# An mLSTM layer's input projections as one-level Strassen block products on eight Trainium2 cores

## What is computed

```python
u = jnp.einsum("bsd,de->bse", x, w_in)       # w_in: 2048 x (2*1024 + 3*2048 + 16)
qk, v, o, z, gates = jnp.split(u, ...)
qk = jax.nn.silu(_causal_depthwise_conv(qk, conv_w, conv_b))   # width 4 along tokens
h = _mlstm_chunkwise(qh, kh, vh, ig_h, lf_h)  # 8 heads, key 128, value 256: recurrence over tokens
h = hc * lax.rsqrt(jnp.mean(hc * hc, axis=-1, keepdims=True) + LN_EPS)   # per head, hc = h - mean
h = h * head_g
h = jax.nn.sigmoid(o) * h * jax.nn.silu(z)    # the gates
y = jnp.einsum("bse,ed->bsd", h, w_out)
x = _layernorm(ALPHA * x + y, ln_g, ln_b)
```

## Time and profile before

| | |
|---|---|
| runs shown, median (lowest to highest) | 2603.67 us (2599.31 to 2607.32) |
| span of the profiled execution, slowest core (all eight) | 2594.3 us (2582.3 to 2594.3) |
| TensorE, VectorE, GpSimd, ScalarE busy | 97%, 61%, 41%, 34% |
| first layer's projections end, second layer begins | 970.65 us, 1192.60 us |

### The profile page before, as it was taken

How to read it: one execution, slowest core, us unless ns; L and a number is a source line. 1 busy time by engine, 2 the same in 40 slices (tenths; PEclk the granted TensorE clock), 3 DMA queues, 4 the chain that set the end, 5 groups by cost and what they waited for, 6 DMA issues and landing times.

```text
span 2594.3 us, 38771 instructions; the slowest of 8 cores (2582.3 to 2594.3 us)
## 1 busy us (share of the span) xinstructions
PE 2526.9 (97%) x13315; PEld 1274.2 (49%) x13315; DVE 1593.5 (61%) x2805; ACT 891.8 (34%) x1573; POOL 1052.5 (41%) x1006
## 2 busy tenths in 40 slices
PE   7999999999999999999899999999999999998997
PEld 3565555555555664444444444444444444443443
DVE  3755555555655555664676666666666777645665
ACT  2423333333333321322344443434334444421111
POOL 3333333333333222433554545454445555442533
PEclk9999999999999999999999999999999999999999
DMA  9878769595966469984455555655555555676762
GB/s 158 136 122 118 107 96 131 84 130 79 134 94 96 107 124 211 229 226 120 103 110 115 107 104 107 115 102 108 109 113 107 118 110 103 131 182 172 249 217 82
DMA packets 473742, 335.06 MB, mean 129 GB/s; under 512 B 413520, under 2 KB 446416, under 8 KB 461776
## 3 DMA queue, kind: packets, MB, share of 16 engines
q1 hardware_dynamic: 451984, 197.25, 34.9%
q0 software_dynamic: 21568, 135.35, 30.1%
HBM read 273.86 MB, written 92.27 MB: 141 GB/s over the span
## 4 chain that ended last, share of the span: by engine, by line
PE 91%; DVE 3%; DMA 2%; POOL 1%; issue 1%; SPq 1%; ACT 1%; DVEq 0%; ACTq 0%; POOLq 0%
PE PSA L892 31%; PE PSA L566 26%; PE PSA L731 15%; PE PSA L518 6%; PE PSA L1058 4%; PE PSA L973 4%; PE PSA L506 1%; DMA REGX<-x_t 1%; DVE REGW L1000 1%; SPq L161 1%; DMA REGX<-REGW 1%; PE PSA L619 1%; PE PSA L617 1%; POOL REGW L756 1%; PE PSA L623 1%
## 5 line engine op out<-in xcount | busy, mean ns | idle before, releaser
L892 PE MATMUL PSA<-REGH,REGX 128*128 128x512 bf16 x4096 | 978.9, 380 | 6.5 <-DVE REGW L899 6.5
L1000 DVE TENSOR_TENSOR_SCAN REGW<-PSA,REGW 128x512 f32<-128x512 f32 (+3 forms) x640 | 682.9, 1091 | 289.6 <-ACT PSA L978 235.3
L566 PE MATMUL PSA<-REGH,REGX 128*128 128x256 bf16 (+1 forms) x4096 | 701.7, 326 | 0.0
L1026 POOL TENSOR_TENSOR REGW<-REGW 128x1024 bf16<-128x1024 f32 (+7 forms) x384 | 527.4, 1391 | 329.9 <-DVE REGW L1000 177.1
L892 PEld LDWEIGHTS PSA<-REGH,REGX 128*128 128x128 bf16 x4096 | 397.8, 98 | 465.0 <-issue 12.6
L566 PEld LDWEIGHTS PSA<-REGH,REGX 128*128 128x128 bf16 x4096 | 395.8, 98 | 229.6
L978 ACT ACTIVATE PSA<-PSA 128x512 f32<-128x512 f32 (+3 forms) x640 | 327.0, 519 | 287.9 <-PE PSA L973 281.3
L904 ACT CAST REGW<-PSA 128x512 bf16<-128x512 f32 x192 | 112.6, 586 | 351.9 <-PE PSA L892 348.5
L973 PE MATMUL PSA<-REGW 128*128 128x512 bf16 (+3 forms) x640 | 220.9, 350 | 8.3 <-DVE REGW L1000 8.3
L731 PE MATMUL PSA<-REGH,REGX 128*128 128x512 bf16 x1024 | 225.7, 383 | 2.0 <-DVE REGW L734 1.1
L731 PE MATMUL PSA<-REGX,REGW 128*128 128x512 bf16 x1024 | 222.0, 379 | 1.3 <-DVE REGW L734 1.3
(11 more groups left out here) (121 smaller groups left out, 1954.3 us busy)
## 6 DMA issues: line engine op xcount, KB each, us to landing
REGX<-wb POOLq DMA_DIRECT2D x64, 512.0 KB, 4.3
y<-REGW SPq DMA_DIRECT2D x26, 1024.0 KB, 5.6
REGH<-a_wv POOLq DMA_DIRECT2D x32, 768.0 KB, 18.2
wb<-kv_w POOLq DMA_DIRECT2D x32, 512.0 KB, 10.7
wb<-b_w_in POOLq DMA_DIRECT2D x32, 512.0 KB, 9.1
REGW<-y SPq DMA_DIRECT2D x14, 1024.0 KB, 7.7
REGW<-x SPq DMA_DIRECT2D x13, 1024.0 KB, 7.0
REGH<-a_wqk POOLq DMA_DIRECT2D x16, 512.0 KB, 26.6
```

What stands on the lines that cost most here:

```text
L566: yield Op("pe", lambda: P_.matmul(PS[bank][:, 0:n1 - n0], lhsT=XT[tb][:, c, t0:t0 + 128], rhs=WV[par][:, c, n0:n1], start=(c == 0), stop= ...
L892: yield Op("pe", lambda c=c: P_.matmul(PS[bank], lhsT=WS[i % 4][:, c, :], rhs=X1[tb][:, c, :], start=(c == 0), stop=(c == KC - 1)), R=[f"W ...
L1000: yield Op("dve", lambda: V.tensor_tensor_scan(out=RR[slot][:, lo:hi][:, ::-1], data0=PS[bank][:, 0:w][:, ::-1], data1=mk[:, ::-1], initia ...
L1026: yield Op("pool", lambda: G.tensor_tensor(out=AA[:, (pos + b0) * 128:(pos + b1) * 128], in0=RR[slot][:, lo + 1:hi + 1], in1=RR[slot][:, l ...
```

## The change

- **Block products.** q, k, v, o, z all come channel-major, in pairs of 128-channel units: per head the pairs are (q, k), (v, v), (o, z), (o, z). A pair `w` with two token blocks is a 2 x 2 block product over the two halves of the 2048 channels, and `grp` makes it from seven products of 8 chunks x 512 columns instead of eight. Head 0's first two pairs stay plain (`plain`).
- **Sums.** `xsum` makes the sums of x once per token pair (and negates and subtracts in place). `wsum` makes five sums of 1024 elements for each pair of weight units, on GpSimd. `gev` evacuates a group: two copies on ScalarE, five 512-wide operations on VectorE.
- **v** is written in bf16 to four buffers `VTa` and transposed by SP's DMA into `VN` (`vtr`); the input-gate weight goes onto k instead (`knw`, ScalarE) and into the mask multiplication.
- **Gates.** `gat` makes them channel-major, with head_g, and writes them to DRAM (`gda`). The norm's last two VectorE operations become one; the gates are loaded beside the transposed mixed tile and multiplied on it by VectorE (`agm`).
- **Out-projection weights** are cast to bf16 in DRAM first (16 more casts) and loaded by `awo`; its PSUM banks go from two to five.
- Single buffers for q, k (`QTa`, `KTa`, `KN`), six `U`, four `HB` instead of eight; the scratch for GpSimd's DMA descriptors is set to 4096.

```diff
+        GL = []
+        for h in range(NH_A):
+            if h == 0:
+                GL += [(0, 2, 0), (0, 2, 1), (0, 3, 0), (0, 3, 1)]
+            elif h < NH_A - 1:
+                GL += [(h, pr, p) for pr in range(4) for p in range(2)]
+            else:
+                GL += [(h, 0, 0), (h, 0, 1), (h, 1, 0), (h, 1, 1), (h, 2, 0), (h, 3, 0), (h, 2, 1), (h, 3, 1)]
...
+            for w in range(2, NW):
+                yield lambda: w < 3 or w - 3 in wd
+                yield from wu(w, 0)
+                yield from wu(w, 1)
+
+        def xsum():
+            for p in range(2):
...
+                for out, i0, i1, op in ((fx(0), b11, b22, ALU.add), (fx(2), b21, b11, ALU.subtract), (fx(1), b12, b22, ALU.subtract)):
+                    yield Op("dve", lambda: V.tensor_tensor(out=out[0], in0=i0[0], in1=i1[0], op=op), R=i0[1] + i1[1], W=out[1],
+                             cost=2.3, first=True)
+                for x in (b22, b11):
+                    yield Op("act", lambda: A_.activation(out=x[0], in_=x[0], func=AF.Copy, scale=-1.0), R=x[1], W=x[1], cost=3.6,
+                             first=True)
+                e, E, x = ("dve", V, 2.3) if p else ("pool", G, 7.5)
+                for out, i1 in ((b21, b22), (b12, b11)):
+                    yield Op(e, lambda: E.tensor_tensor(out=out[0], in0=out[0], in1=i1[0], op=ALU.subtract), R=i1[1], W=out[1],
+                             cost=x, first=True)
...
+        def wsum():
+            for w in range(2, NW):
+                yield lambda: at("wu") >= 2 * w + 1 and (w < 4 or w - 2 in wd)
+                a11, a12, a21, a22 = half(w, 0, 0), half(w, 0, 1), half(w, 1, 0), half(w, 1, 1)
+                for out, i0, i1, op in ((ew(w, 0), a11, a22, ALU.add), (ew(w, 1), a11, a12, ALU.add), (ew(w, 2), a21, a22, ALU.add),
+                                        (a12, a12, a22, ALU.subtract), (a21, a21, a11, ALU.subtract)):
+                    yield Op("pool", lambda: G.tensor_tensor(out=out[0], in0=i0[0], in1=i1[0], op=op), R=i0[1] + i1[1], W=out[1],
+                             cost=1.9)
...
-                yield lambda: at("vz") >= 6 + 1.25 * i
-                yield Op("pool", None, cost=3.0, dma=dict(slot="cast", out=out, in_=in_))
+                yield lambda: at("gp") >= 2 + 0.56 * i
+                yield Op("pool", None, cost=3.0, dma=dict(slot="casta" if i < 16 else "cast", out=out, in_=in_))
...
+        def grp():
+            for n, (h, pr, p) in enumerate(GL):
+                w, a, b = 4 * h + pr, 2 * p, 2 * p + 1
+                bz, bx, by = [(3 * n + i) % 5 for i in range(3)]
...
+                prods = ((ew(w, 0), fx(0), bz, True), (half(w, 1, 1), fx(2), bx, True), (half(w, 0, 0), fx(1), by, True),
+                         (ew(w, 1), xq(b, 1), bx, False), (ew(w, 2), xq(a, 0), by, False), (half(w, 0, 1), xq(a, 1), bx, False),
+                         (half(w, 1, 0), xq(b, 0), by, False))
+                need = (7 * n - 8, 7 * n - 8, 7 * n - 7, 7 * n + 1, 7 * n + 2, 7 * n + 3, 7 * n + 4)
+                for i, (wo, xo, bank, fresh) in enumerate(prods):
+                    yield lambda: at("ge") >= need[i] and at("wsum") >= w and at("xsum") >= p and 1 in wd
+                    for c in range(8):
+                        yield Op("pe", lambda: P_.matmul(PS[bank], lhsT=wo[0][:, c, :], rhs=xo[0][:, c, :], start=(fresh and c == 0),
+                                                         stop=(c == 7), skip_group_check=True), R=wo[1] + xo[1], W=[("ps", bank)],
+                                 inc=(c == 7), cost=0.216, slack=0.3)
...
+        def gev():
...
+                yield Op("act", lambda: A_.copy(out=m1, in_=PS[bz]), R=[("ps", bz)], W=[mk_], cost=0.58, first=True)
...
+                yield Op("act", lambda: A_.copy(out=ag, in_=PS[bx]), R=[("ps", bx)], W=[gk_], cost=0.58, first=True)
...
+                yield Op("dve", lambda: V.tensor_tensor(out=ag, in0=PS[by], in1=ag, op=ALU.add), R=[("ps", by), gk_], W=[gk_],
+                         cost=0.69, first=True)
...
+                for k, (u, tb, bank, sub) in enumerate(((0, b, bx, True), (1, a, by, True), (0, a, bx, False), (1, b, by, False))):
...
+                        yield Op("dve", lambda: V.tensor_tensor(out=out, in0=ag, in1=PS[bank], op=ALU.subtract),
+                                 R=[gk_, ("ps", bank)], W=[key], cost=0.69, first=True)
...
+        def vtr():
...
+                    yield lambda: (h, 1, u, tb) in uqd and (h == 0 or at("recm") >= 16 * (h - 1) + 4 * tb + 3)
+                    yield Op("sp", None, R=[("VTA", tb % 2, u)], W=[("VN", tb, u)], cost=1.0,
+                             dma=dict(slot=f"vn{tb}{u}", out=VN[:, 4 * tb:4 * tb + 4, u * 128:(u + 1) * 128],
+                                      in_=VTa[:, tb % 2, u, :], transpose=True))
...
+                    yield Op("act", lambda: A_.activation(out=gs, in_=vz, func=AF.Sigmoid), R=[("U", uz)], W=[sk], cost=0.64)
+                    yield Op("act", lambda: A_.activation(out=vo, in_=vo, func=AF.Sigmoid), R=[("U", uo)], W=[("U", uo)], cost=0.64)
+                    yield Op("dve", lambda: V.scalar_tensor_tensor(out=gs, in0=vz, scalar=PRT[:, 80 + c:81 + c], in1=gs, op0=ALU.mult,
+                                                                   op1=ALU.mult), R=[("U", uz), "PRT"], W=[sk], cost=0.77)
...
+                    yield Op("pool", lambda: G.tensor_tensor(out=g16, in0=gs, in1=vo, op=ALU.mult), R=[sk, ("U", uo)], W=[gk],
+                             cost=1.28)
...
+                    yield Op("sp", None, R=[gk], W=[("GD", tb, c)], cost=0.6,
+                             dma=dict(slot=f"gd{x % 2}", out=gda[c, :, tb * 512:(tb + 1) * 512], in_=g16))
...
+                yield Op("dve", lambda: V.tensor_scalar(out=HB[i % 4], in0=PS[b][:, 0:256], scalar1=s(4), scalar2=s(3),
+                                                        op0=ALU.subtract, op1=ALU.mult),
+                         R=[("ps", b), sk(4), sk(3)], W=[("HB", i % 4)], cost=0.43)
...
+                yield lambda: at("agm") >= t - 3 and (NW - 2, NW - 2, NW - 1)[min(t, 2)] in wd and at("gat") >= (62 if t < 8 else 64)
...
+                yield Op("sp", None, R=[("GD", t // 4, c) for c in range(KC)], W=gtk[g], cost=3.0,
+                         dma=dict(slot=f"gt{g}", out=GTA[g], in_=gda[:, :, t * 128:(t + 1) * 128].rearrange("c p t -> p c t")))
...
+                yield Op("dve", lambda: V.tensor_tensor(out=MGA[t % 4], in0=MGA[t % 4], in1=GTA[t % 3], op=ALU.mult),
+                         R=gtk[t % 3], W=agk[t % 4], cost=1.25, first=True)
```

More of the change, by code:

```diff
@@ L344, in build @@
         WG = wt(0.5, [KC, 16], BF16, ["WG"])
-        SST = wt(0.125, [2, 16], F32, ["SST"])
-        assert o <= 76.5, o
-        U += [tile("H", 40 + 2.0625 * i, [528], F32, [("U", 4 + i)]) for i in range(4)]
+        assert o <= 84.5, o
         def consts():
@@ L414, in build @@
         ncast = [0]
         def casts():
-            src = []
+            src = [(wao16[nb, p:p + 32], a_w_out[nb, p:p + 32]) for nb in range(4) for p in range(0, 128, 32)]
             for h in range(NH_B):
@@ L460, in prologue @@
[L460 to L463 removed]
+            yield Op("pe", lambda: P_.transpose(out=PS[7][:, 0:128], in_=AL, identity=ID32[:]), R=["AL", "ID32"],
+                     W=[("ps", 7)], cost=0.25, slack=0.3)
@@ L598, in recf @@
+                yield Op("act", lambda: A_.activation(out=KNW[i % 3], in_=KN[:, t, :], func=AF.Copy,
+                                                      scale=WW[:, 8 * t + h:8 * t + h + 1]),
+                         R=[knk[t // 4], "WW"], W=[("KNW", i % 3)], cost=0.35, first=True)
+                st["knw"] = i
         def recf():
```

494 lines of the change are left out of this document (265 added, 229 removed).

## The result

The changed kernel takes 2763.84 us (median), the kernel before 2601.64 us beside it: a ratio of 1.0595, 95% interval 1.0549 to 1.0641. One of its four runs, 3075.72 us, fell into a slower state of the chip and is not in the ratio. I had predicted 2576 us and a range up to 2634. It is slower, and by more than any case that I had put a time to (2646 us).

The account below looks back on a forecast made before the run. TensorE alone was taken to bound the kernel up to 970 us, VectorE after the change. -48 (heads) + 8 (hand-over) + 12 (out-projection) = -28 us on 2594.3 gave 2566, plus 9.4 for the median 2576 us; range 2510 to 2634.

Parts of the forecast that it names:

- TensorE's saving: First-layer heads: TensorE needs 102.6 us a head instead of 116.8; 106 us in all if nothing else gave way.
- VectorE's need: First-layer heads: 92 us of VectorE operations plus 18 us of waiting for GpSimd, 110 us a head.
- the exclusion: Heads: VectorE operations with two SBUF inputs and GpSimd instructions reading SBUF block each other; 18 us a head, ends 0 and 54.
- VectorE needs 110 us a head ... and sets the pace: Heads 1 to 7: VectorE, above TensorE's 102.6 us, sets the pace; 6.8 us less per head, 48 us over seven.
- 93% at 110: Heads: DMA has 102.5 us of transfers a head, 93% of a head of 110 us.
- Rival 2: Heads: a v tile waits for its buffer, VectorE stands and TensorE stops; ten us a head give 2646 us; chance 0.31.
- Head 0 I take at nothing: Start-up: head 0 was counted as neither gain nor loss.
- ends +7 and -15: Head 0: 7 us gained by its grouped pairs; some 15 lost if block sums of x take 5.5 us each.
- Hand-over and out-projection: End of layer one: 8 us lost waiting for the last gates (ends 0 and 15), 12 by gate loads (8 to 18).
- The clock: Heads: read as 1.00 between 200 and 800 us before the change; the sum has no term for it.

Follow-up runs that it names:

- f4: The changed kernel, every engine's order kept, with later weight sums, v transposes from head 1 on and 60 of 96 casts all made nearly free; ratio 1.0067.
- f3: The changed kernel, every engine's order kept, with 60 of the 96 casts moving one row of 128 instead of all; ratio 1.0368.
- c1: The changed kernel with 64 plain products per group, no weight or x sums, and the buffers of the kernel before given back; ratio 1.0454.
- d2: The changed kernel with 64 plain products per group and no sums, its planner taking k and v transposes to land 9 us later; ratio 1.0719.
- g2: The changed kernel, all work done, with 20 casts instead of 96; the second layer loads its other weights as f32 when used; ratio 1.0386.
- g1: As g2, with the 150 weight sums on VectorE instead of GpSimd and four gate tiles instead of two; ratio 1.0322.
- f1: The changed kernel, every engine's order kept, with each GpSimd weight sum from the fifth unit on a memset of two columns; ratio 1.0354.

## Why the prediction was wrong, by its own steps

**TensorE's saving: right.** 102.6 us a head is what f4 runs at from head 3 to head 6.

**VectorE's need: right in sum.** In f3 VectorE is busy 368.2 us in 400, and 400 us are 1725 / 511 = 3.38 heads: 109 us a head, where I had 92 + 18 = 110. The parts were off both ways. By means over 200 to 900 us in f3 (1.276, 1.307 and 0.637 us against 0.752, 0.752 and 0.183) the exclusion costs 24 x 0.52 + 8 x 0.56 + 16 x 0.45 = 24 us, and the rest is 85. The exclusion was too small mostly because a sum costs 2.16 us and not 1.89; with 2.16 in the prediction's formula GpSimd's arithmetic is 73 us, the length met 1.70 us, half of it less 0.2 is 0.65, and 48 x 0.71 x 0.65 = 22 us.

**"VectorE needs 110 us a head ... and sets the pace": the step that failed.** It takes VectorE to be full. It isn't, not even with short landings (92% in f3, 118 us a head), and in the changed kernel it is at 83% and a head takes 127.2: VectorE, TensorE, GpSimd, ScalarE and SP run in order and stand at each other's results. I had DMA in the sum only as a rate, 102.5 us a head, "93% at 110", and the waits for its landings at nothing. Those are its cost: three kinds of transfer that a head's chain now hangs on (v transposes, gate writes, k transposes without a spare copy) land behind 14 casts a head, and with the casts cheap (f3) the kernel gains 59 us.

**Rival 2 named the mechanism and not its size.** The buffer that the v tile waits for, VectorE standing at it, TensorE behind it, SP's queue: all are in the timeline at 234 to 267 us. I gave it ten us a head on top of the 110, and 2646 us in all; measured are seventeen on top of the 110, and a start-up that it didn't have. I set it beside the forecast with a chance of 0.31 and put nothing of it into the sum. In the kernels with plain products the v tiles as such aren't the place, and TensorE's first recurrence product of a head is: that shows in c1 and d2. In the changed kernel TensorE stands at both, 14.4 and 35.6 us.

**"Head 0 I take at nothing", ends +7 and -15: failed.** Start-up lost 77 us, where the sum gave it only the 7 us that head 0's groups save. It wasn't the block sums of x, on which the -15 stood: they take 2.28 us each on VectorE and not 5.5. Two stands of TensorE in the changed kernel's timeline are 37 of them: 17.55 us at 124 us behind a chain of VectorE that the sums hold up (last section), and 19.75 us at 267 us behind the v tile. In g2, with fewer casts, the first recurrence product of head 1 comes at 239.7 us instead of 273.5; in g1, with the sums on VectorE too, at 220 on core 6. These two have orders of their own, so they only agree with it. In f1, with the order kept, it comes 14 us earlier.

**Hand-over and out-projection: one right, one low.** From the last group product, which ends at 1099.99 us, to the first of the out-projection are 10 us (forecast 8). The out-projection lost 25 us on the slowest core, and 19 in the median of the others; I had 12, ends 8 and 18. The reason that I gave, gate loads on a full DMA, fits the 1.00 of that stage and VectorE's 22.6 us, but wasn't tested apart from the multiplication, which takes 1.22 us in the median of its 16.

**The clock was no term at all.** Between 400 and 800 us it is granted at 0.94 instead of 1.00; in f4, where TensorE doesn't stop, at 1.00. Of the matmuls between 104 and 1106 us some 150 start about 0.43 us after the one before, double the 0.2155 of 2.4 GHz, so at 1.2 GHz, and nearly all of them right behind a stretch in which TensorE had stood: 150 x (0.43 - 0.2155) = 32 us, which the sum should have added to the waits. The plainest case is the first, in the timeline:

```profile
123.63 1.19 PE L514 MATMUL PSA<-REGW,ONE 1*128 1x128 f32 x4 [17.55 <-DVE REGW L511]
124.75 6.39 PE L588 MATMUL PSA<-REGX,REGW 128*128 128x512 bf16 x17
```

TensorE had stood for 17.55 us, and 17 products take 6.39 us instead of 17 x 0.2155 = 3.7; from 124 to 134 us the clock is granted at 0.70.

## What to carry to other kernels

Work that moves off a full engine onto others with room is not paid in their busy time alone: ask which transfers now lie inside the loop's chain, take their landing time under the traffic that is really there, and add up causes that hold at once instead of choosing among them. Where a planner writes the order, taking a part out changes everything else as well; keep the order and make the part nearly free, and the gains can be compared and added, here within their intervals. Where the queues beside the saved engine are as full as here (DMA at 0.76 before the change), count what they have to give up first: the 106 us of products saved came out as no gain even in f4, which leaves most of that other work out.
